# Making the half-width operands of a three-pass matmul kernel in three pieces instead of one block

## The reference, cut to what matters

```python
def rmsnorm(x, g):
    y = x * lax.rsqrt(jnp.mean(x * x, axis=-1, keepdims=True) + EPS)
    return y * g

def swiglu(x, w_gu, w_down):                       # D_MODEL = 1024, D_FF = 2816
    g, u = jnp.split(x @ w_gu, 2, axis=-1)
    return (jax.nn.silu(g) * u) @ w_down

x = x + 0.5 * swiglu(rmsnorm(x, norm_ffn1_g), ffn1_w_gu, ffn1_w_down)
x = x + hybrid_mixer(rmsnorm(x, norm_mix_g), ...)
x = x + 0.5 * swiglu(rmsnorm(x, norm_ffn2_g), ffn2_w_gu, ffn2_w_down)
x = rmsnorm(x, final_norm_g)
...                                                # attention and retention
h = rms_norm(x, norm_mlp)
x = x + jnp.square(jax.nn.relu(h @ w_up)) @ w_down # w_up 1024 x 4096
```

## Time and profile before

| what | value |
|---|---|
| median of three runs | 1864.93 us (1863.07 to 1865.03) |
| the profiled execution | 1863.93 us, its span 1861.6 us |
| TensorE matmuls busy | 1796.7 us, 97% |
| TensorE weight loads busy | 1553.1 us, 83% |
| VectorE busy | 1190.1 us, 64% |
| ScalarE busy | 814.2 us, 44% |
| DMA traffic | 176.54 MB, mean 95 GB/s |
| mean granted clock of TensorE | 0.986 of full |

### The profile page before, as it was taken

How to read it: one execution, slowest core, us unless ns; L and a number is a source line. 1 busy time by engine, 2 the same in 40 slices (tenths; PEclk the granted TensorE clock), 3 DMA queues, 4 the chain that set the end, 5 groups by cost and what they waited for, 6 DMA issues and landing times.

```text
span 1861.6 us, 25522 instructions
## 1 busy us (share of the span) xinstructions
PE 1796.7 (97%) x10056; PEld 1553.1 (83%) x10056; DVE 1190.1 (64%) x1842; ACT 814.2 (44%) x1338; POOL 37.7 (2%) x37
## 2 busy tenths in 40 slices
PE   8799999999999999999969999999999988999998
PEld 6689989878888888888759998988877876989887
DVE  7756948647765534455676694875677566747474
ACT  5344626444332223323434462554656432637273
POOL 0000000000000000000000000000222000000000
PEclk9899999999999999999979999999999999999999
DMA  4232333332123332323213233234421322233231
GB/s 153 65 114 89 105 102 103 98 115 80 57 92 95 96 102 90 102 91 101 68 57 122 82 105 112 96 105 131 134 65 48 99 69 91 80 102 106 88 114 68
DMA packets 65942, 176.54 MB, mean 95 GB/s; under 512 B 7952, under 2 KB 9232, under 8 KB 65824
## 3 DMA queue, kind: packets, MB, share of 16 engines
q1 hardware_dynamic: 63984, 171.60, 29.4%
q10 hardware_dynamic: 1424, 2.14, 0.3%
q0 software_dynamic: 416, 1.18, 0.2%
HBM read 170.70 MB, written 2.10 MB: 93 GB/s over the span
## 4 chain that ended last, share of the span: by engine, by line
PE 81%; DVE 10%; ACT 5%; issue 3%; DMA 0%; ACTq 0%; DVEq 0%
PE ps L1844 17%; PE ps L1846 17%; PE ps L1845 17%; PE ps L1918 7%; PE ps L1921 7%; PE ps L1920 7%; PE ps L1866 2%; PE ps L1868 2%; PE ps L1867 2%; DVE wl L1055 1%; ACT wh L522 1%; DVE BTlo L1116 1%; DVE wl L1062 1%; DVE Alo L1185 1%; ACT wh L532 1%
## 5 line engine op out<-in xcount | busy, mean ns | idle before, releaser
L1918 PE MATMUL ps<-BThi,wh 128*128 128x256 f32 x1316 | 371.2, 282 | 25.9 <-DVE BTlo L1116 20.3
L1920 PE MATMUL ps<-BTlo,wh 128*128 128x256 f32 x1316 | 369.0, 280 | 0.0
L1921 PE MATMUL ps<-BThi,wl 128*128 128x256 f32 x1316 | 369.0, 280 | 0.0
L1055 DVE TENSOR_TENSOR wl<-raw,wh 128x1024 fp32r<-128x1024 f32 (+1 forms) x224 | 271.0, 1210 | 141.9 <-ACT wh L522 140.1
L522 ACT ACTIVATE wh<-raw 128x1024 fp32r<-128x1024 f32 (+1 forms) x224 | 231.8, 1036 | 238.9 <-PE ps L1846 202.0
L1844 PE MATMUL ps<-Hhi,wh 128*128 128x512 f32 x768 | 311.3, 405 | 20.3 <-DVE wl L1055 20.2
L1844 PE MATMUL ps<-Ahi,wh 128*128 128x512 f32 x792 | 310.4, 392 | 10.5 <-DVE Alo L1185 9.5
L1845 PE MATMUL ps<-Alo,wh 128*128 128x512 f32 x792 | 309.1, 390 | 0.0
L1846 PE MATMUL ps<-Ahi,wl 128*128 128x512 f32 x792 | 308.9, 390 | 0.0
L1845 PE MATMUL ps<-Hlo,wh 128*128 128x512 f32 x768 | 302.6, 394 | 0.0
L1846 PE MATMUL ps<-Hhi,wl 128*128 128x512 f32 x768 | 302.4, 394 | 0.0
(11 more groups left out here) (306 smaller groups left out, 2074.1 us busy)
## 6 DMA issues: line engine op xcount, KB each, us to landing
raw<-in_w_gu SPq DMA_DIRECT2D x140, 256.0 KB, 2.9
raw<-in_w_d SPq DMA_DIRECT2D x32, 512.0 KB, 3.5
raw<-in_w_dn SPq DMA_DIRECT2D x32, 512.0 KB, 3.8
raw<-in_w_up SPq DMA_DIRECT2D x48, 256.0 KB, 2.8
raw<-in_w_gu SPq DMA_DIRECT2D x16, 512.0 KB, 3.5
raw<-in_w_d SPq DMA_DIRECT2D x16, 384.0 KB, 3.1
raw<-in_w_v SPq DMA_DIRECT2D x8, 512.0 KB, 4.0
raw<-in_w_cc SPq DMA_DIRECT2D x8, 512.0 KB, 3.8
```

The costliest lines, as they stand in the source:

```text
L1055: dve.tensor_tensor(WL[WS[u]][:, 0:n], RAW[RSL[u]][:, 0:n], f32(WH[WS[u]][:, 0:n]), ALU.subtract).then_inc(s["wl"], 1)
L1918: pe.matmul(ps, whi[:, w], BThi[:, c, kp, :], start=(new and kp == 0), stop=False, skip_group_check=not new)
L1920: pe.matmul(ps, whi[:, w], BTlo[:, c, kp, :], start=False, stop=False, skip_group_check=not new)
L1921: last = pe.matmul(ps, wlo[:, w], BThi[:, c, kp, :], start=False, stop=(kp == 3), skip_group_check=not new)
```

## The change

The slice work is cut in three pieces: `normed` (two instructions), `sums_of_blocks` (four) and `low_blocks` (one). In `ffn` the norm piece of slice kp stands after feed(u+3), ahead of VectorE's wait for the up unit; the sums stand behind the product L1220 and ahead of Alo; the low piece of the slice before stands between times_r of the gate and the wait for silu. ScalarE's copy comes last in its step, behind the copy to Ahi. All of it moves into the last ordinary steps, one slice a step, and there is one ordinary step more in each of the two feed-forwards (JS from (5, 4) to (6, 5)), so 45 pairs instead of 47. In the mlp one piece stands in each up unit from j = 1, between the ReLU product L1735 and Alo, and the rest in the first four down units. Merge 1 goes ahead of the low part in mlp pairs, and the last low parts of a group go ahead of `feed(u+2)` of the first down unit. A scratch tile of the pair sums changes its place (`sums_of`).

```diff
@@ -58,7 +58,7 @@
         self.eng.wait_ge(self.sem, self.n)
 
 
-JS = (5, 4)
+JS = (6, 5)
 NP = 7
 
 UNITS = []
@@ -410,7 +410,7 @@
         return (u >= U0["ffn2"]) + (u >= U0["mlp"])
 
     def sums_of(p):
-        return SS[:, :], SS2[:, :], TA[8], (TA[7], TA[6], SW3[:, :])[layer(p)]
+        return SS[:, :], SS2[:, :], TA[8], (TA[6], TA[7], SW3[:, :])[layer(p)]
 
     def part(p, c):
 
@@ -418,8 +418,8 @@
         return (RAWP[RSL[p][1]], s1, s2, RAWP[RSL[p][3]], s3, s4, RAWP[RSL[p][2]])[c]
 
     MLP_UP = [U0["mlp"] + 16 * g for g in range(4)]
-    BUILD = [{2: 0, 4: 1, 6: 2, 7: 3}, {1: 0, 3: 1, 4: 2, 6: 3}, {2: 0, 4: 1, 6: 2, 8: 3}]
-    BUILT = [{3: 0, 5: 1, 7: 2, 8: 3}, {2: 0, 4: 1, 5: 2, 7: 3}, {3: 0, 5: 1, 7: 2, 9: 3}]
+    BUILD = {1: ("norm", 0), 2: ("sums", 0), 3: ("low", 0), 4: ("norm", 1), 5: ("sums", 1), 6: ("low", 1), 7: ("norm", 2)}
+    BUILD_DN = {0: (("sums", 2),), 1: (("low", 2), ("norm", 3)), 2: (("sums", 3),), 3: (("low", 3),)}
     MLP_DN = [U0["mlp"] + 16 * g + 8 for g in range(4)]
     GU, DN = {}, {}
     for f in (0, 1):
@@ -601,14 +601,12 @@
                     if f == 1 and j == 0:
                         norm(6)
                     silu(u, j)
-                    if 2 * j in BUILD[f]:
-                        operands(f, BUILD[f][2 * j])
                     if f == 1 or j > 1:
                         feed(u + 3)
                     act.wait_ge(s["ev"], EVN[u + 1])
                     act.activation(Ahi[:, j - a, :], TA[6 + j % 2], ACT.Copy).then_inc(s["ah"], 1)
-                    if 2 * j + 1 in BUILD[f]:
-                        operands(f, BUILD[f][2 * j + 1])
+                    if JS[f] - 5 <= j < JS[f] - 1:
+                        operands(f, j - JS[f] + 5)
                 first = max(a, JS[f])
                 for j in range(first, b):
                     p, v = GU[f, g] + 2 * (j - a), GU[f, g] + 2 * (j - a) + 2
@@ -950,8 +948,8 @@
                     norm(11)
                 act.wait_ge(s["upv"], j + 1)
                 act.activation(Ahi[:, j, :], TA[2 + j % 2], ACT.Copy).then_inc(s["ah"], 1)
-                if j in BUILD[2]:
-                    operands(2, BUILD[2][j])
+                if j in BUILD and BUILD[j][0] == "sums":
+                    operands(2, BUILD[j][1])
             for j in range(0, 8, 2):
                 if g == 0:
                     break
@@ -994,8 +992,8 @@
                 if g == 3 and n == 5:
                     act.preload_act_table_set(LN_SET)
                 feed(u + 2)
-                if g == 0 and 8 + n in BUILD[2]:
-                    operands(2, BUILD[2][8 + n])
+                if g == 0 and n in (0, 2):
+                    operands(2, 2 + n // 2)
                 if g == 3:
                     act.wait_ge(s["ev"], EVN[u])
                     square(n)
@@ -1091,7 +1089,7 @@
             else:
                 lo(u)
 
-        def operands(i, kp):
+        def normed(i, kp):
 
 
             g = ("g1", "g2", "gl2")[i]
@@ -1103,6 +1101,8 @@
             for dst, k in ((BF[:, 0:8:7, :], kp), (BF[:, 3:6:2, :], kp + 4)):
                 own.add(dve.scalar_tensor_tensor(out=dst, in0=X[:, k, :].rearrange("p (h t) -> p h t", h=2),
                                                  scalar=vc(g, k), in1=halves, op0=ALU.mult, op1=ALU.mult))
+
+        def sums_of_blocks(i, kp):
             own.wait()
             own.add(dve.tensor_tensor(BF[:, 1, :], BF[:, 7, :], BF[:, 0, :], ALU.subtract))
             own.add(dve.tensor_tensor(BF[:, 4, :], BF[:, 5, :], BF[:, 7, :], ALU.subtract))
@@ -1111,16 +1111,19 @@
             own.wait()
             dve.tensor_tensor(BF[:, 6, :], BF[:, 3, :], BF[:, 2, :], ALU.subtract).then_inc(s["bf"], 1)
 
-        def operands_lo(i, kp):
+        def low_blocks(i, kp):
             dve.wait_ge(s["bh"], 4 * i + kp + 1)
             dve.tensor_tensor(BTlo[:, :, kp, :], BF[:, 0:NP, :], f32(BThi[:, :, kp, :]),
                               ALU.subtract).then_inc(s["bl"], 1)
 
-        def build(i, step):
-            if step in BUILT[i]:
-                operands_lo(i, BUILT[i][step])
-            if step in BUILD[i]:
-                operands(i, BUILD[i][step])
+        def build(step):
+            what, kp = step
+            if what == "norm":
+                normed(2, kp)
+            elif what == "sums":
+                sums_of_blocks(2, kp)
+            else:
+                low_blocks(2, kp)
 
         def merge(p, i, dst):
 
@@ -1187,6 +1190,8 @@
         def ffn(f, after, sums):
             def gate(u, j):
                 times_r(u, TA[j % 2])
+                if JS[f] - 5 < j:
+                    low_blocks(f, j - JS[f] + 4)
                 dve.wait_ge(s["silu"], f * FT + j + 1)
                 own.add(dve.tensor_tensor(TA[4 + j % 2], TA[2 + j % 2], R[:, :], ALU.mult))
 
@@ -1212,16 +1217,18 @@
                     if f == 1 and j == 0:
                         norm(6, 3)
                     gate(u, j)
-                    build(f, 2 * j)
                     if f == 1 or j > 1:
                         feed(u + 3)
+                    if JS[f] - 5 <= j < JS[f] - 1:
+                        normed(f, j - JS[f] + 5)
                     dve.wait_ge(s["pe"], PEN[u + 1])
                     own.wait()
                     dve.tensor_tensor(TA[6 + j % 2], BK[BANK[u + 1]][:, :], TA[4 + j % 2],
                                       ALU.mult).then_inc(s["ev"], 1)
+                    if JS[f] - 5 <= j < JS[f] - 1:
+                        sums_of_blocks(f, j - JS[f] + 5)
                     dve.wait_ge(s["ev"], EVN[u + 1])
                     a_lo(38 * f + a, j - a, TA[6 + j % 2])
-                    build(f, 2 * j + 1)
                 first = max(a, JS[f])
                 for j in range(first, b):
                     p, v = GU[f, g] + 2 * (j - a), GU[f, g] + 2 * (j - a) + 2
@@ -1255,9 +1262,9 @@
                 product(p, b - 1)
                 for n in range(KT):
                     u = DN[f, g] + n
-                    feed(u + 2)
                     if n == 0:
                         a_lo(38 * f + a, b - 1 - a, TA[4])
+                    feed(u + 2)
                     dve.wait_ge(s["pe"], PEN[u])
                     dve.scalar_tensor_tensor(out=X[:, n, :], in0=BK[BANK[u]][:, :], scalar=0.5, in1=X[:, n, :],
                                              op0=ALU.mult, op1=ALU.add).then_inc(s["ev"], 1)
@@ -1734,9 +1741,10 @@
                 dve.wait_ge(s["ev"], EVN[u])
                 dve.scalar_tensor_tensor(out=TA[2 + j % 2], in0=TA[j % 2], scalar=0.0, in1=TA[j % 2], op0=ALU.max,
                                          op1=ALU.mult).then_inc(s["upv"], 1)
+                if j in BUILD:
+                    build(BUILD[j])
                 dve.wait_ge(s["upv"], j + 1)
                 a_lo(60, j, TA[2 + j % 2])
-                build(2, j)
             for j in range(0, 8, 2):
                 if g == 0:
                     break
@@ -1755,9 +1763,9 @@
                     pair_lo(v, 1)
                 else:
                     lo(v)
+                merge(p, 1, TA[6][:, LEFT])
                 if j > 0:
                     a_lo(60 + 8 * g, j - 1, TA[7])
-                merge(p, 1, TA[6][:, LEFT])
                 if v in PAIR:
                     pair_lo(v, 2)
                     total(v, 2)
@@ -1769,12 +1777,12 @@
                     lo(v + 1)
             for n in range(KT - (g == 3)):
                 u = MLP_DN[g] + n
-                feed(u + 2)
                 if g > 0 and n == 0:
                     a_lo(60 + 8 * g, 6, TA[4])
                     a_lo(60 + 8 * g, 7, TA[7])
-                if g == 0:
-                    build(2, 8 + n)
+                feed(u + 2)
+                for step in BUILD_DN.get(n, ()) if g == 0 else ():
+                    build(step)
                 add_x(u, n)
                 if g == 3:
                     add_square(n, 48, 42)
```

## The result

The changed kernel takes 1819.52 us (median of four, 1818.65 to 1822.95) where the kernel before takes 1864.28 (median of four, 1863.07 to 1865.03): a ratio of 0.976 with a 95% interval from 0.975 to 0.978. The forecast was 1820.8.

The account below looks back on a forecast made before the run. VectorE, by its waits, bound the stretches where slices are made. First feed-forward 10.3, second 15.6, mlp group 0 14.0, last two parts 2.4 and 1.8: 44.1 us off 1863.93, plus 1.0 for the median, 1820.8; range 1813 to 1832.

Parts of the forecast that it names:

- The loop: Feed-forward steps with a slice: VectorE's step falls from 14.1 to 11.9 us against TensorE's 10.9, leaving about 1 us wait.
- The third products: First pair of each feed-forward: third product held by ScalarE's queued tap, starting at 87.9 in the first, 959.0 in the second.
- The price of the low clock: Each feed-forward's pair start: the wait before the third product may leave a low clock, costing 0 to 1.9 us, middle 1.0.
- Mlp group 0: Slices spread over three units each: last Alo at 1538.4 instead of 1550.95, and no low clock after it; gain 14.0 us.
- The last two parts: Mlp: last Alo ahead of feed gains 2.4 us (nothing in ffn); merge 1 ahead of Alo gains 1.8 us.
- The banks: Banks and slots turn by one or two places; next users wait for old evictions: nothing, or up to 1 us.
- TensorE's waits: Totals fall: BTlo from 20.3 to 4 to 8 us, wl from 20 to 5 to 8, Alo to about 2, merges about 3.
- A: Rival: about ten short waits left in the stretches each leave half clock, costing 8 us more: 1829 us; 14%.
- D: Rival: the clock stays at its lower level through the stretches because waits come at every step: slower, 1902 us; 3%.
- B: Rival: waits only change their name, a step stays near 14 us: about 1854 us, or 1838 if half is kept; 8%.
- C: Rival: no low clock at the third product (-2.0) and no mlp wait for merges (-2.5): 1816 us; 13%.
- E: Rival: no visible change; the walk would have to be wrong by 40 us; 1%.

Follow-up runs that it names:

- The two experiments on either side: The changed kernel with ScalarE's copy to BThi ahead of its copy to Ahi, 1824.72 us; with ScalarE's weights ahead of the copy to BThi, 1803.43 us.
- the first experiment: The kernel before with only one more ordinary step in each feed-forward, every order as before: 1859.55 us, 0.9975.

## Why the prediction was right, point by point

**The total.** 1820.8 against 1819.52. By the landmarks of the profiled execution the 40.3 us are: first feed-forward 8.6, the way from there to the second 1.0, second feed-forward 14.3, the nv projection -1.2, mlp group 0 14.7, the rest 4.8, and -1.9 for the late start. Without the late start that is 42.2 for a forecast of 44.1, so the terms together came out 1.9 too large in this execution. The medians lie 44.8 apart, 2.5 more: 1.5 because the other executions of the changed kernel were faster than the late start explains, 0.7 outside the spans, and 0.3 because the median of before lies that much above its profiled execution (the forecast added 1.0 for this). So the total agrees better than its terms do, in part by luck.

Two more traces show the changed lists up to mlp group 0: the kernel with merge 1 back and the one with useless work differ from the changed kernel only behind it. From R to the restart in mlp group 0 the changed kernel takes 1488.6 us, these two 1487.6 and 1486.0. All of this spread stands behind the two third products: from there to the first down unit 19.4, 18.6 and 18.4 us in the first feed-forward, 28.8, 28.7 and 27.2 in the second. So the same lists pay a different price for the low clock from one execution to the next, and the 1.5 us are of this size.

**The loop.** Right to a few hundredths: 11.92 for 11.9, idle only ahead of wl, and ScalarE waits for BF alone. The two experiments on either side (12.45 and 9.71) show that it is this loop that carries the time. The loop says a wait of 1 us a step; in the second feed-forward one of 0.75 stands before 930.63 and none other above 0.2. In the first there is none: behind the 3.29 us wait 24 matmuls took 8.3 us where they take 5.6 behind a wait at full clock, so TensorE was late by more than the loop in the next two steps. A wait that was counted beside the low clock was inside it.

**The third products.** Forecast 87.9, with the late start 89.8; it came at 90.16. The second, walked with the shift as measured up to there, should have come at 951.3; it came at 951.79. Both 0.4 to 0.5 late. What held them is not ScalarE's tap, as the prediction had it, but the third product's low weights: VectorE makes them from 89.42 (in the kernel before from 88.21), directly behind Alo, and Alo waits 0.77 us for ScalarE's copy to Ahi. The distance read from the rows was right, its reason was not.

**The price of the low clock was the term that was too small in this execution.** It stood at 1.0 us a start (0 to 1.9). In the first feed-forward 12 products from 90.16 took 19.36 us where 17.0 were worked out: 2.3. In the second 19 products from 951.79 took 28.77 where 27.0 were worked out: 1.8. The low clock ahead of the third product there (0.56 from 944.8) cost nothing: the third product comes 7.06 us after the first in both feed-forwards, with a clock of 1.00 between them in the first, since VectorE and ScalarE set that distance. The late third products and this price make 8.6 of the forecast 10.3 and 14.3 of 15.6. In the two other traces the price was 1.5 and 1.3 in the first feed-forward, 1.7 and 0.3 in the second. The closing sentence, that the prediction is wrong if the clock falls below 1.00 in the pairs after the starts, goes against its own term of 0 to 1.9: the clock did fall, for 5.0 and for 3.4 us, and the forecast stood.

**Mlp group 0.** The last Alo was forecast at 1538.4. TensorE restarts on it at 1517.56; with the 20.80 us by which everything had moved forward, that is 1538.36. No low clock behind its 1.43 us: from 1518 to 1556 the clock is 1.00. 14.7 for 14.0.

**The last two parts** were forecast at 2.4 + 1.8 = 4.2. In mlp groups 1 to 3 they brought 4.3 together, but the agreement is luck: the last Alo brought 3.1 and merge 1 then 1.1. (The 4.8 of the rest has 0.5 more, at the very end of the kernel, which neither accounts for.) Three steps failed. The price of a wait was read from its bracket, 0.83 us, and a wait costs 0.3 more than its bracket. The two edits were priced apart, and merge 1 alone is worth nothing, as the table above shows. And "in ffn it gains nothing: no wait stands there" misread: the row of Alo counts six waits, the mlp has four of them, and the other two, of 0.20 us, stand in the feed-forwards. Taking the order of Alo back costs 4.3 in the mlp and 1.4 in the feed-forwards; the other 0.8 of the 6.5 us is seen in the medians alone. The statement on the loop over ScalarE held.

**The banks.** "Nothing, or up to 1 us": one of them cost 1.38, and turning them back removed it. The statement that the next users wait for evictions that are one unit and more old missed one. It isn't in the sum.

**TensorE's waits.** BTlo (forecast 4 to 8) 5.2, Alo (about 2) 1.4, merges (about 3) none that the list shows, with 1.8 for the taps in their place; wl (5 to 8) 10.6, because the second wait of each pair start goes by the name of wl and the restart at 45.17 still had its 3.29.

**The rivals.** A (short waits cost clock) and D (the clock stays low) fall: waits up to 2.27 us left 1.00, four of about 1 us in a row too. What is true in A is that the four waits over 2.4 us of the changed kernel were followed by a low clock. B (the waits change their name) is what happened in the first experiment, where the loop stayed at 14.1, and not in the change, where it didn't. C (no low clock at the third products, no wait for merges left) had both halves wrong: the clock fell, and though the merges left the list, six waits for taps took their place and the 2.5 us did not come; it took Alo behind merge 2 to get there. E is excluded by the result.

**Left open.** From the first mlp pair to the last down unit the kernel with useless work takes 36.6 us more than the changed kernel. 23.8 of them are its waits, some 4.5 the 0.3 us apiece that the brackets leave out, and 8 the five stretches of low clock. What decides whether a wait of 2.4 to 2.9 us is followed by a low clock stays open. So does the late start: between 6 and 10 us TensorE does 9 matmuls in the changed kernel and 17 in the kernel before, that is, it works at half the pace for longer, but the view prints a granted clock of 1.00 there for both, so that this is the clock isn't shown.

## What to carry to other kernels

Where two engines hand work back and forth in fixed lists, walk one round of the loop and compare its length with that of the engine that should set the pace: the same instructions made a round of 14.1, 11.9 or 9.7 us here by their order alone. Put a piece that is ready into each place where the list waits, and on the helper engine put what the other side waits for next (the weights) ahead of what it needs a step later (the copy). A saving that is read from a small wait is a lower bound only: here each such wait cost 0.3 us more than its bracket, and it is measured from an arrival that the other edits bring forward. Price two edits around the same wait together.

## What the runs showed of the hardware

From 20 us on, waits of TensorE up to 2.27 us (0.3, 0.86 to 1.06, 1.43, 1.55) left the granted clock at 1.00 in these traces, four waits of 1 us in a row too. Waits of 2.44 us and more (2.80, 2.81, 2.92, 3.17, 3.29, 3.96) were mostly followed by 3 to 6 us near half, but two, of 2.89 and 2.91 us, were not. (In the first 20 us one wait of 1.92 us, at 7.11 in the kernel before with the extra steps, had a low clock behind it.) The price did not go with the length: behind the wait of 3.29 us near 45 us, 24 full-width matmuls took 8.3 us in the changed kernel and 7.2 in the one with merge 1 back, whose list is the same there, where they take 5.6 at full clock, so 1.6 or 2.7 us on top of the wait.

A wait of TensorE for a full-width unit cost 0.3 us more than its bracket (0.20, 0.83 and 1.12 us in brackets lengthened their groups by 0.5, 1.1 and 1.4).

On VectorE a 128x512 product or difference is followed by the next 0.60 us after its start when the two are independent, and 0.72 us after it when the next one waits for its result; the shown length of both is 0.68 to 0.69.
